# FFN stages of a two-layer hybrid block: another order of the weight splits and low parts on GpSimd, of a tile's turn on TensorE and its norm on VectorE, and its high part cast by ScalarE

## The chip, the cores and the metric

One Trainium2 chip, one core of it. The metric is the device time of one execution in microseconds (us), the median of three runs. TensorE, VectorE, ScalarE, GpSimd and SyncE are called PE, DVE, ACT, POOL and SP in the profile's rows; PEld is TensorE's loading of its stationary operand. SP only issues transfers here.

## The reference

A block of two layers over 1024 latent tokens and 256 context tokens of width 1024. The first part of a layer (three kinds of attention) isn't touched. The second part is the feed-forward sublayer (FFN), hidden width 2816, which ends in a norm; the next layer's input is then normalised and modulated:

```
def swiglu_sublayer(h, shift, scale, gate, w_g, w_u, w_d, g, b):
    u = modulate(h, shift, scale)
    f = (jax.nn.silu(u @ w_g) * (u @ w_u)) @ w_d
    return post_norm(h, f, gate, g, b)          # layer_norm(DN_ALPHA * h + gate * f, g, b)

# next layer: modulate(h, m[0], m[1]) = ln_plain(h) * (1 + m[1]) + m[0]
```

Layer 0 does this for all 1280 tokens (10 tiles of 128), layer 1, the last, for the 1024 latent ones (8 tiles), and has no next layer.

## The kernel before, in words

**Products.** Every matrix product is made of three fp32r products: each operand is split into a high part (a cast to fp32r) and a low part (the value minus its high part), and high x high, high x low and low x high are summed in PSUM (lines 131 to 133, in `product`). So each tile of weights, 128x1024 floats, is loaded by SP into one of two slots of `ring_raw` (line 2555), cast by ACT into one of three slots of `ffn_whi` (line 2634), and subtracted by POOL into `ffn_wlo` (line 2758). Both are called `split` in the code, and run in one fixed order, the list `order`. The load of a tile of weights waits for POOL's split two places earlier in that list; ACT's cast waits until PE is through with the tile three places earlier.

**Stage.** `swiglu` runs 22 groups q (G = 11 per pass, two passes over the weights). A pass takes one set of tokens: the first 768 (layer 0) or 512 (layer 1), the second the last 512. A group takes 256 hidden columns: two halves f, each with a gate tile (`GATE[f]`) and an up tile (`UPPER[f]`) of weights, and two tiles of the down product (`DOWN[0]`, `DOWN[1]`). PE runs in each group: gate and up of half 0, the down product of the group before (`down(q - 1)`, which waits for both of its splits), gate and up of half 1. The gate goes through silu on ACT (2642), is multiplied by up on DVE (2926) and split by POOL into hidden high and low parts (2765, 2767). The down products of 4 tiles x 2 halves are added into `y` by DVE (2934, 2938), through two PSUM banks `ffn_acc`; PE waits when DVE is behind in emptying them.

**Norms.** The tiles of the first pass are complete when the second begins, and are normalised beside it, one in each of the groups G + 1, 2, 4, 5, 7, 8 (layer 0; six tiles) or G + 1, 2, 4, 5 (layer 1; four): `norm_tile(q)` names it. Groups G + 1, 4, 7 are called here the first of a pair, G + 2, 5, 8 the second. The steps of tile k:
- DVE `residual(k)`: y times gate (2894), plus the residual (2900), statistics (2875, 2877); `shifted(k)`: minus the mean, times gain (2908), reciprocal (2883), times that plus bias (2911), and in layer 0 statistics again; `normalizers(k)` (2883, 2888).
- ACT, between them: two roots (`deviation(k, 0)` and `(k, 1)`, 2648), and in layer 0 `normalize(k)` into `ffn_x` (2656).
- PE (layer 0): `turn(k)`, eight transposes (2810), then ACT `modulate(k)`, eight activations (2661), DVE `high_part(k)` (2919), POOL `low_part(k)` (2772) into the next stage's operand `second_uhi`, `second_ulo`. `normalize(k + 1)` waits for `low_part(k)`, since both use `ffn_x`.

Two further tiles, from the stage before, are normalised in groups 0 and 1 of each stage (`late_norm` on DVE, lines 2942 to 2966, `late_low_part` on POOL, 2753).

**Where each step stands.** The order on each engine is written out by hand, in one loop over q per engine. Before the change: DVE runs in group q the high part of the tile of group q - 1, then residual, shifted and normalizers of its own tile, then the multiplication of half 0, the eight additions of the down product and the multiplication of half 1. POOL runs the low part (late or not) of the tile before, then the split of `DOWN[1]` of group q - 1, then `GATE[1]`, hidden, `UPPER[1]`, the next group's first two splits, hidden and `DOWN[0]`. PE turns the tile between the down product and half 1. ACT runs both roots and `normalize` ahead of the casts of half 1, and `modulate` behind the cast of the next group's `GATE[0]` and ahead of the silu of half 1. SP's order of loads, residual loads (2563) and stores (2569, which wait for `h_done`) is not touched.

The wait that PE has at the head of the down product:

```
pe.wait_ge(*split_done(weight(q, DOWN[1])))
for n, (c, tt, at) in enumerate(tiles_of(q)):
    pe.wait_ge(hid_ready, unit(q, 1, c) + 1)
    for half in range(2):
        y = y_count(q, n, half)
        if y > 2:
            pe.wait_ge(y_added, y - 2)
```

Of the kernel before, what the change touches and what calls it, by code (L numbers as in the profile page):

```python
# [22 lines left out]
P = 128  # L23
LAYERS = 2
D = 1024
KT = D // P
# [2392 lines left out]
def swiglu(nc, t, res, layer, last):  # L2419
    with nc.cleanup_on_exit(), ExitStack() as ctx:  # L2420
# [73 lines left out]
        def x_of(k):  # L2494
            return xs[(k - NT) % 2] if k >= NT else x
# [48 lines left out]
        def norm_tile(q):  # L2544
            return group_of.index(q - G) if q - G in group_of else None
# [76 lines left out]
        def _(act):  # L2622
# [35 lines left out]
            def modulate(k, parts=range(KT)):  # L2658
# [3 lines left out]
                                       scale=scale[:, stream(k), i:i + 1], bias=shift[:, stream(k), i:i + 1])  # L2662
                m.then_inc(u_done, 1)

            def late_deviation(k, j):
                act.wait_ge(late_mean_done, 2 * k + j + 1)
                if k:
                    act.wait_ge(late_rs_done, 2 * (k - 1) + j + 1)
                act.activation(late_sd[:, j:j + 1], late_mean[:, j, 1:2], ACT.Sqrt, bias=eps[:, 0:1]).then_inc(late_sd_done, 1)
# [21 lines left out]
            for q in range(Q):  # L2691
                k = norm_tile(q)
                turning = k is not None and not last
                silu(q, 0)
                if 0 < q < Q - 1:
                    split(q - 1, DOWN[1])
                if q < LATE:
                    if q:
                        late_deviation(q, 0)
                    late_deviation(q, 1)  # L2700
                    late_normalize(q)
                if k is not None:
                    deviation(k, 0)
                if turning:
                    deviation(k, 1)
                    normalize(k)
                split(q, GATE[1])
                split(q, UPPER[1])
                if q + 1 < Q:
                    split(q + 1, GATE[0])  # L2710
                if q < LATE:
                    late_modulate(q)
                if turning:
                    if k == 0:
                        act.wait_ge(one_plus, 1)
                    modulate(k)
                silu(q, 1)
                if q + 1 < Q:
                    split(q + 1, UPPER[0])
                if q < Q - 2:  # L2720
                    split(q, DOWN[0])
            for q in range(Q - 2, Q):
                split(q, DOWN[0])
                split(q, DOWN[1])

            def high_part(k):
                at = slice(all_tiles[k] * P, (all_tiles[k] + 1) * P)
                act.wait_ge(u_done, k + 1)
                if k == NT + NL - 1:
                    act.wait_ge(u_rest, 1)  # L2730
                act.copy(uhi[:, :, at], x_of(k)[:, :].rearrange("p (k n) -> p k n", k=KT)).then_inc(u_hi, 1)

            for m in range(NL):
                k = NT + m
# [12 lines left out]
        def _(pool):  # L2747
# [27 lines left out]
            if not last:  # L2775
                for st in range(2):
                    for dst, at in ((shift, 0), (scale, 1)):
                        pool.dma_start(dst[:, st, :], t["mod"][layer + 1, 1 - st, at * D:(at + 1) * D].rearrange("(k p) -> p k", p=P)).then_inc(const_in, 16)
            for q in range(Q):
                if 0 < q <= LATE:  # L2780
                    late_low_part(q - 1)
                if not last and norm_tile(q - 1) is not None:
                    low_part(norm_tile(q - 1))
                if 0 < q < Q - 1:
                    split(q - 1, DOWN[1])
                split(q, GATE[1])
                hidden(q, 0)
                split(q, UPPER[1])
                if q + 1 < Q:
                    split(q + 1, GATE[0])  # L2790
                    split(q + 1, UPPER[0])
                else:
                    split(q - 1, DOWN[0])
                    split(q - 1, DOWN[1])
                hidden(q, 1)
                if q < Q - 2:
                    split(q, DOWN[0])
# [4 lines left out]
        def _(pe):  # L2802
# [49 lines left out]
            for q in range(Q):  # L2852
                if q == G:
                    pe.wait_ge(late_lo, LATE)
                gate_and_up(q, 0)
                if 0 < q < Q - 1:
                    down(q - 1)
                if q < LATE:
                    late_turn(q)
                if norm_tile(q) is not None and not last:  # L2860
                    turn(norm_tile(q))
                gate_and_up(q, 1)
            down(Q - 2)
            down(Q - 1)
            if not last:
# [5 lines left out]
        def _(dve):  # L2871
# [29 lines left out]
                dve.wait_ge(summed, k + 1)  # L2901
                statistics(k, 0)

            def shifted(k):
                y = Y[:, all_tiles[k], :]
                dve.wait_ge(ln_in, 32)
                dve.wait_ge(mv_done[0], k + 1)
                dve.scalar_tensor_tensor(y, y, mv[:, 0, 0:1], lng[:, :], ALU.subtract, ALU.mult).then_inc(centered, 1)  # L2908
                inverse(k, 0)
                dve.wait_ge(centered, k + 1)  # L2910
                dve.scalar_tensor_tensor(y, y, rstd[:, 0:1], lnb[:, :], ALU.mult, ALU.add).then_inc(h_done, 1)  # L2911
                if not last:
                    dve.wait_ge(h_done, k + 1)
                    statistics(k, 1)

            def high_part(k):
                at = slice(all_tiles[k] * P, (all_tiles[k] + 1) * P)
                dve.wait_ge(u_done, k + 1)
                dve.tensor_copy(uhi[:, :, at], x[:, :].rearrange("p (k n) -> p k n", k=KT)).then_inc(u_hi, 1)

            def multiply(q, f):
                for c, (t0, tn) in enumerate(chunks_of(q, f)):
# [47 lines left out]
            for q in range(Q):  # L2970
                k = norm_tile(q)
                if q < LATE:
                    late_norm(q)
                if q == LATE and not last:
                    dve.wait_ge(const_in, 64)
                    dve.tensor_scalar(scale[:, :, :], scale[:, :, :], 1.0, None, ALU.add).then_inc(one_plus, 1)
                if not last and norm_tile(q - 1) is not None:
                    high_part(norm_tile(q - 1))
                if k is not None:
                    residual(k)  # L2980
                    shifted(k)
                    if not last:
                        normalizers(k)
                multiply(q, 0)
                if 0 < q < Q - 1:
                    for n in range(len(tiles_of(q - 1))):
                        accumulate(q - 1, n)
                multiply(q, 1)
            for n in range(len(tiles_of(Q - 2))):
                accumulate(Q - 2, n)  # L2990
# [6 lines left out]
            for m in range(NL + 1):  # L2997
                k = NT + m
                if m < NL:
                    accumulate(Q - 1, m)  # L3000
                if m and not last:
                    normalizers(k - 1)
                if m < NL:
                    residual(k)
                    shifted(k)
                if 0 < m < NL and not last:
                    if m == NL - 1:
                        normalizers(k)
                        low_part(k - 1)
                        break  # L3010
                    low_part(k - 1)
# [161 lines left out]
```

## Time and profile before

| what | value |
|---|---|
| the three runs | 3757.8, 3759.4, 3764.65 us; median 3759.4 us |
| span of the profiled execution, first to last instruction | 3757.6 us |
| busy, share of the span | PE 91%, PEld 75%, DVE 44%, POOL 43%, ACT 39% |
| mean granted TensorE clock over the span | 0.955 of full speed |

The profiled execution is shown by its span; the time around it (launch and end) has no row of its own, and the median of the runs is 1.8 us above that span. The two FFN stages are the stretches from about 1110 to 2100 us (layer 0; its second pass from 1660 us on) and from about 2990 us to the end (layer 1). A row of the timeline reads: start and duration in us, engine, line and operation, what it writes and reads, the number of instructions merged, and in brackets how long the engine was idle before it and what ended that. A row of a stretch gives each engine's busy time and number of instructions in it, the granted clock, and the share and rate of the transfers. Matmul ends are modelled, and spans on POOL are rough.

### The profile page before, as it was taken

The numbers are of one execution on the slowest core, as the hardware profiler recorded it, in microseconds if no ns is written. First come the engines' busy times: TensorE is split into PE (matmuls) and PEld (weight loads), VectorE is DVE, ScalarE is ACT, GpSimd is POOL, SyncE is SP. The second block draws the span as 40 slices with busy tenths as digits, with TensorE's granted clock in tenths as the row PEclk, the third lists the DMA queues.
The fourth block names the chain that finished last, engine by engine and source line by source line (L and its number), as shares of the span: only waits on it lengthen the run. The fifth ranks groups of instructions, "written<-read, shape, count | busy, mean of one in ns | idle before, by whom it ended". The sixth has DMA issues, their size and how long they took to land. (4 is left out here: it accounts for less than half of the span.)

```text
span 3757.6 us, 52063 instructions
## 1 busy us (share of the span) xinstructions
PE 3418.3 (91%) x20432; PEld 2826.1 (75%) x20432; DVE 1635.7 (44%) x2527; ACT 1452.5 (39%) x2346; POOL 1612.1 (43%) x1002
## 2 busy tenths in 40 slices
PE   5998987989789999999998799888897899999996
PEld 4987885666578888887776688786665778888885
DVE  4045546856562122224443218548664622224414
ACT  4151766855343111113332333558753432222221
POOL 3011425933235344346654202338632365556652
PEclk8999996989999999999999899998998999999998
DMA  5243501455442111223323234521454332233332
GB/s 208 81 146 139 148 24 54 89 175 167 146 124 98 66 62 64 66 68 113 117 96 106 96 109 151 168 57 53 118 150 150 124 123 96 96 97 117 118 101 84
DMA packets 209630, 409.86 MB, mean 109 GB/s; under 512 B 20192, under 2 KB 114752, under 8 KB 208896
## 3 DMA queue, kind: packets, MB, share of 16 engines
q1 hardware_dynamic: 187344, 381.22, 32.0%
q10 hardware_dynamic: 20480, 21.32, 1.8%
q0 software_dynamic: 1584, 4.24, 0.3%
q8 instruction: 154, 2.52, 0.3%
q14 instruction: 68, 0.56, 0.0%
HBM read 331.20 MB, written 75.51 MB: 108 GB/s over the span
## 5 line engine op out<-in xcount | busy, mean ns | idle before, releaser
L2758 POOL TENSOR_TENSOR ffn_wlo<-ring_raw,ffn_whi 128x1024 fp32r<-128x1024 f32 x262 | 638.0, 2443 | 702.3 <-ACT ffn_whi L2634 701.5
L2634 ACT CAST ffn_whi<-ring_raw 128x1024 fp32r<-128x1024 f32 x264 | 273.0, 1051 | 833.1 <-PE ffn_acc L133 469.4
L2926 DVE TENSOR_TENSOR ffn_silu<-ffn_up,ffn_silu 128x512 f32<-128x512 f32 x110 | 70.1, 637 | 879.9 <-PE ffn_up L133 866.9
L131 PE MATMUL ffn_acc<-ffn_whi,ffn_hhi 128*128 128x512 f32 x792 | 318.2, 402 | 49.5 <-DVE y L2938 24.6
L2938 DVE TENSOR_TENSOR y<-ffn_acc,y 128x512 f32<-128x512 f32 x360 | 248.1, 691 | 252.3 <-PE ffn_acc L133 252.3
L131 PE MATMUL ffn_gate<-second_uhi,ffn_whi 128*128 128x512 f32 (+1 forms) x880 | 326.9, 371 | 22.0 <-DVE ffn_wlo L2969 20.9
L132 PE MATMUL ffn_gate<-second_ulo,ffn_whi 128*128 128x512 f32 (+1 forms) x880 | 325.8, 370 | 0.0
L133 PE MATMUL ffn_gate<-second_uhi,ffn_wlo 128*128 128x512 f32 (+1 forms) x880 | 325.3, 370 | 0.0
L131 PE MATMUL ffn_up<-second_uhi,ffn_whi 128*128 128x512 f32 (+1 forms) x880 | 324.0, 368 | 0.0
L132 PE MATMUL ffn_up<-second_ulo,ffn_whi 128*128 128x512 f32 (+1 forms) x880 | 323.9, 368 | 0.0
L133 PE MATMUL ffn_up<-second_uhi,ffn_wlo 128*128 128x512 f32 (+1 forms) x880 | 323.7, 368 | 0.0
L132 PE MATMUL ffn_acc<-ffn_wlo,ffn_hhi 128*128 128x512 f32 x792 | 316.7, 400 | 0.0
L133 PE MATMUL ffn_acc<-ffn_whi,ffn_hlo 128*128 128x512 f32 x792 | 315.1, 398 | 0.0
L131 PEld LDWEIGHTS ffn_acc<-ffn_whi,ffn_hhi 128*128 128x128 f32 x792 | 153.3, 194 | 87.8 <-issue 28.8
L2373 DVE TENSOR_SCALAR_CACHE_REDUCE diff_scores<-diff_scores 128x1280 f32<-128x1280 f32 (+1 forms) x144 | 196.8, 1382 | 25.1 <-PE diff_scores L2234 19.9
L131 PEld LDWEIGHTS ffn_gate<-second_uhi,ffn_whi 128*128 128x128 f32 x880 | 167.0, 190 | 50.7 <-DVE ffn_wlo L2969 21.4
L2642 ACT ACTIVATE ffn_silu<-ffn_gate 128x512 f32<-128x512 f32 x110 | 61.2, 558 | 370.5 <-PE ffn_gate L133 370.4
L2351 POOL TENSOR_TENSOR diff_w<-diff_w,diff_e 128x1280 f32<-128x1280 f32 (+1 forms) x72 | 192.0, 2667 | 6.0
L2303 ACT ACTIVATE diff_e<-diff_scores,diff_negmax 128x1280 f32<-128x1280 f32 (+1 forms) x144 | 178.6, 1240 | 36.9 <-DVE diff_scores L2373 35.9
L1914 POOL TENSOR_SCALAR swa_p<-swa_p,swa_rden 128x640 f32<-128x640 f32 (+1 forms) x144 | 107.3, 764 | 193.3 <-DVE swa_rden L2089 193.3
L132 PEld LDWEIGHTS ffn_gate<-second_ulo,ffn_whi 128*128 128x128 f32 x880 | 167.1, 190 | 28.0
L133 PEld LDWEIGHTS ffn_gate<-second_uhi,ffn_wlo 128*128 128x128 f32 x880 | 167.1, 190 | 28.0
(332 smaller groups left out, 7979.0 us busy)
## 6 DMA issues: line engine op xcount, KB each, us to landing
ring_raw<-w_ffn_dram SPq DMA_DIRECT2D x264, 512.0 KB, 3.5
swa_ada_w<-w_ada_dram SPq DMA_DIRECT2D x20, 2048.0 KB
gla_kq<-proj_scratch SPq DMA_DIRECT2D x32, 320.0 KB, 7.7
local_qhl<-heads_scratch SPq DMA_DIRECT2D x36, 256.0 KB, 7.6
norm_attention_mix<-mix_scratch SPq DMA_DIRECT2D x18, 512.0 KB, 5.3
h_mid_scratch<-late_h SPq DMA_DIRECT2D x18, 512.0 KB, 5.2
first_ada_w<-w_ada_dram SPq DMA_DIRECT2D x4, 2048.0 KB
in_w_raw<-w_in_dram SPq DMA_DIRECT2D x15, 512.0 KB, 5.7
```

The costliest lines, as they stand in the source:

```text
L131: pe.matmul(out, st_hi, mv_hi, start=start, stop=False)
L132: pe.matmul(out, st_hi, mv_lo, start=False, stop=False)
L133: return pe.matmul(out, st_lo, mv_hi, start=False, stop=stop)
L1914: pool.tensor_scalar(pr[:, m % RING, j, 0:keys], pr[:, m % RING, j, 0:keys], rden[:, m % RING, j:j + 1], 1.0, ALU.mult, ALU.mult).then_inc ...
L2303: act.activation(E[:, r % 4, c, 0:keys], SC[:, c, 0:keys], ACT.Exp, bias=ng[:, c:c + 1], scale=-1.0, accum_out=den[:, c, tile_of(i, r), r ...
L2351: pool.tensor_tensor(w, w, E[:, u % 4, 0, 0:keys], ALU.add).then_inc(w_done, 1)
L2373: dve.tensor_scalar(SC[:, c, 0:keys], SC[:, c, 0:keys], -scale, 3e38, ALU.mult, ALU.min, accum_out=ng[:, c:c + 1]).then_inc(neg_done, 1)
L2634: act.copy(whi[:, w % 3, :], raw[:, w % 2, :]).then_inc(w_hi, 1)
L2642: act.activation(sg[:, n % 2, 0:tn], GT[:, n % 2, 0:tn], ACT.Silu).then_inc(silu_done, 1)
L2758: pool.tensor_tensor(wlo[:, w % 3, :], raw[:, w % 2, :], whi[:, w % 3, :].bitcast(F32), ALU.subtract).then_inc(w_ready, 1)
L2926: dve.tensor_tensor(sg[:, n % 2, 0:tn], UP[:, n % 2, 0:tn], sg[:, n % 2, 0:tn], ALU.mult).then_inc(mul_done, 1)
L2938: dve.tensor_tensor(Y[:, tt, cols], ACC[:, half, :], Y[:, tt, cols], ALU.add).then_inc(y_added, 1)
```

## The change: what it does

- **POOL:** the split of `DOWN[1]` of the group before stands first in a group, ahead of both kinds of low part; the low part of a normalised tile moves behind the split of `UPPER[1]`.
- **DVE:** `shifted` gives up its first step (2908), now `centre`, which stays behind `residual`, ahead of the multiplication of half 0. The rest of `shifted`, and `normalizers`, move behind the additions of the down product. The high part is gone from DVE.
- **ACT:** the second root and `normalize` move behind the cast of the next group's `GATE[0]`; `modulate` behind the silu of half 1 and the cast of the next `UPPER[0]`; the high part follows it on ACT, ahead of the cast of `DOWN[0]`.
- **PE:** the turn moves behind gate and up of half 1.

```diff
@@ ScalarE
+            def high_part(k):
+                at = slice(all_tiles[k] * P, (all_tiles[k] + 1) * P)
+                act.wait_ge(u_done, k + 1)
+                if k == NT + NL - 1:
+                    act.wait_ge(u_rest, 1)
+                act.copy(uhi[:, :, at], x_of(k)[:, :].rearrange("p (k n) -> p k n", k=KT)).then_inc(u_hi, 1)
...
                 if k is not None:
                     deviation(k, 0)
-                if turning:
-                    deviation(k, 1)
-                    normalize(k)
                 split(q, GATE[1])
                 split(q, UPPER[1])
                 if q + 1 < Q:
...
                 if q < LATE:
                     late_modulate(q)
                 if turning:
+                    deviation(k, 1)
+                    normalize(k)
+                silu(q, 1)
+                if q + 1 < Q:
+                    split(q + 1, UPPER[0])
+                if turning:
                     if k == 0:
                         act.wait_ge(one_plus, 1)
                     modulate(k)
-                silu(q, 1)
-                if q + 1 < Q:
-                    split(q + 1, UPPER[0])
+                    high_part(k)
                 if q < Q - 2:
                     split(q, DOWN[0])
@@ GpSimd
             for q in range(Q):
+                if 0 < q < Q - 1:
+                    split(q - 1, DOWN[1])
                 if 0 < q <= LATE:
                     late_low_part(q - 1)
-                if not last and norm_tile(q - 1) is not None:
-                    low_part(norm_tile(q - 1))
-                if 0 < q < Q - 1:
-                    split(q - 1, DOWN[1])
                 split(q, GATE[1])
                 hidden(q, 0)
                 split(q, UPPER[1])
+                if not last and norm_tile(q - 1) is not None:
+                    low_part(norm_tile(q - 1))
                 if q + 1 < Q:
                     split(q + 1, GATE[0])
                     split(q + 1, UPPER[0])
@@ TensorE
                 if q < LATE:
                     late_turn(q)
+                gate_and_up(q, 1)
                 if norm_tile(q) is not None and not last:
                     turn(norm_tile(q))
-                gate_and_up(q, 1)
@@ VectorE
-            def shifted(k):
+            def centre(k):
                 y = Y[:, all_tiles[k], :]
                 dve.wait_ge(ln_in, 32)
                 dve.wait_ge(mv_done[0], k + 1)
                 dve.scalar_tensor_tensor(y, y, mv[:, 0, 0:1], lng[:, :], ALU.subtract, ALU.mult).then_inc(centered, 1)
+
+            def shifted(k):
+                y = Y[:, all_tiles[k], :]
                 inverse(k, 0)
...
-            def high_part(k):
-                at = slice(all_tiles[k] * P, (all_tiles[k] + 1) * P)
-                dve.wait_ge(u_done, k + 1)
-                dve.tensor_copy(uhi[:, :, at], x[:, :].rearrange("p (k n) -> p k n", k=KT)).then_inc(u_hi, 1)
...
-                if not last and norm_tile(q - 1) is not None:
-                    high_part(norm_tile(q - 1))
                 if k is not None:
                     residual(k)
-                    shifted(k)
-                    if not last:
-                        normalizers(k)
+                    centre(k)
                 multiply(q, 0)
                 if 0 < q < Q - 1:
                     for n in range(len(tiles_of(q - 1))):
                         accumulate(q - 1, n)
+                if k is not None:
+                    shifted(k)
+                    if not last:
+                        normalizers(k)
                 multiply(q, 1)
...
                 if m < NL:
                     residual(k)
+                    centre(k)
                     shifted(k)
```

## Rows read from the trace of the kernel before

**Rows 1.** The page: the span and each engine's busy time
```profile
span 3757.6 us, 52063 instructions
PE 3418.3 (91%) x20432; PEld 2826.1 (75%) x20432; DVE 1635.7 (44%) x2527; ACT 1452.5 (39%) x2346; POOL 1612.1 (43%) x1002
```

**Rows 2.** PE's waits, 1690 to 2000 us: releaser, total us, times, longest
```profile
PE ffn_acc L131 <- POOL ffn_wlo L2758: 9.7, 3, 3.2
PE ffn_acc L131 <- DVE y L2938: 2.9, 2, 1.5
PE ffn_acc L131 <- DVE y L2934: 1.5, 1, 1.5
```

**Rows 3.** PE's waits, 3020 to 3060 us (layer 1)
```profile
PE ffn_acc L131 <- POOL ffn_wlo L2758: 4.1, 1, 4.1
```

**Rows 4.** Stretches: down products behind a gap, one without, 10 us around 1695 us
```profile
1733.63:1746.30 12.67, 12.67 (x49) 10.20 (x50) 5.48 (x9) 2.18 (x2) 4.22 (x3) 0.87 0.50 167
...
1946.81:1960.70 13.89, 13.89 (x48) 11.13 (x49) 5.48 (x9) 2.18 (x2) 4.21 (x3) 0.78 0.23 77
3034.12:3046.78 12.66, 12.65 (x48) 10.20 (x49) 5.49 (x9) 2.18 (x2) 4.22 (x3) 0.87 0.40 126
1768.94:1779.82 10.88, 10.88 (x49) 9.01 (x48) 5.53 (x8) 1.06 (x1) 4.25 (x3) 1.00 0.29 99
...
1690.00:1700.00 10.00, 8.55 (x38) 6.82 (x37) 8.66 (x11) 5.16 (x7) 4.47 (x2) 1.00 0.43 157
```

**Rows 5.** Timeline of DVE, first group of a pair (1684 to 1702 us)
```profile
1689.39 2.92 DVE L2908 SCALAR_TENSOR_TENSOR y<-y,ffn_mv,ffn_lng 128x1024 f32<-128x1024 f32 x1
...
1695.69 1.29 DVE L2875 BATCH_NORM_STATS2 ffn_stats<-y 128x6 f32<-128x512 f32 x2
...
1698.46 1.28 DVE L2934 COPY y<-ffn_acc 128x512 f32<-128x512 f32 x2
```

**Rows 6.** Timeline of POOL, second group of a pair (1718 to 1736 us)
```profile
1723.56 3.39 POOL L2758 TENSOR_TENSOR ffn_wlo<-ring_raw,ffn_whi 128x1024 fp32r<-128x1024 f32 x1
1726.91 3.38 POOL L2772 TENSOR_TENSOR second_ulo<-ffn_x,second_uhi 128x1024 fp32r<-128x1024 f32 x1
1730.26 3.32 POOL L2758 TENSOR_TENSOR ffn_wlo<-ring_raw,ffn_whi 128x1024 fp32r<-128x1024 f32 x1
```

**Rows 7.** Timeline of PE: the first matmul behind each of two gaps (two queries)
```profile
1699.29 0.47 PE L131 MATMUL ffn_acc<-ffn_whi,ffn_hhi 128*128 128x512 f32 x1 [1.45 <-DVE y L2934]
...
1733.63 0.50 PE L131 MATMUL ffn_acc<-ffn_whi,ffn_hhi 128*128 128x512 f32 x1 [3.24 <-POOL ffn_wlo L2758]
```

**Rows 8.** Timeline of POOL, first group, splits behind the down product
```profile
1708.90 4.75 POOL L2758 TENSOR_TENSOR ffn_wlo<-ring_raw,ffn_whi 128x1024 fp32r<-128x1024 f32 x2 [4.35 <-ACT ffn_whi L2634]
```

**Rows 9.** Timeline of ACT, the same pair of groups (1706 to 1736 us)
```profile
1709.68 2.90 ACT L2661 ACTIVATE ffn_x<-ffn_tr,ffn_shift,ffn_scale 128x128 f32<-128x128 f32 x8
1712.61 1.28 ACT L2642 ACT_TABLE_LOAD   x1
...
1719.54 1.06 ACT L2634 CAST ffn_whi<-ring_raw 128x1024 fp32r<-128x1024 f32 x1 [3.65 <-PE ffn_up L133]
1724.98 0.60 ACT L2642 ACTIVATE ffn_silu<-ffn_gate 128x512 f32<-128x512 f32 x1 [4.38 <-PE ffn_gate L133]
...
1733.69 1.25 ACT L2656 ACTIVATE ffn_x<-y,ffn_nmu,ffn_rstd 128x1024 f32<-128x1024 f32 x1 [0.42 <-DVE ffn_nmu L2888]
```

**Rows 10.** Timeline of PE: the turn, between the down product and half 1
```profile
1707.58 1.03 PE L2810 MATMUL ffn_tr<-ident,ffn_x 128*128 128x128 f32 x8
1708.37 0.48 PE L131 MATMUL ffn_gate<-second_uhi,ffn_whi 128*128 128x512 f32 x1
```

**Rows 11.** Timeline of DVE, layer 0's tail, POOL idle (2049 to 2058 us)
```profile
2053.61 1.28 DVE L2908 SCALAR_TENSOR_TENSOR y<-y,ffn_mv,ffn_lng 128x1024 f32<-128x1024 f32 x1
```

**Rows 12.** Timeline of POOL, layer 1, group 1 (3022 to 3037 us)
```profile
3028.42 2.37 POOL L2753 TENSOR_TENSOR second_ulo<-ffn_x,second_uhi 128x1024 fp32r<-128x1024 f32 x1
3030.75 3.33 POOL L2758 TENSOR_TENSOR ffn_wlo<-ring_raw,ffn_whi 128x1024 fp32r<-128x1024 f32 x1
```

More of the change, by code:

```diff
@@ L2724, in _ @@
                 split(q, DOWN[1])
-            def high_part(k):
-                at = slice(all_tiles[k] * P, (all_tiles[k] + 1) * P)
[L2728 to L2731, printed above, removed]
             for m in range(NL):
@@ L2914, in shifted @@
                     statistics(k, 1)
-            def high_part(k):
-                at = slice(all_tiles[k] * P, (all_tiles[k] + 1) * P)
-                dve.wait_ge(u_done, k + 1)
-                dve.tensor_copy(uhi[:, :, at], x[:, :].rearrange("p (k n) -> p k n", k=KT)).then_inc(u_hi, 1)
             def multiply(q, f):
```

## The prediction

> **What bounds the kernel now.** I read the page first: PE is busy for 91% of the span and DVE, POOL and ACT for less than half of it each [rows 1], so in the FFN stages only what makes PE wait, or slows its clock, costs time. The tables of PE's waits, taken per stretch, come next, because the change moves work in the second pass of layer 0, in that of layer 1, and in the first groups of both stages. Between 1690 and 2000 us of layer 0 PE waits six times: three times for POOL's split of a down tile, 9.7 us in all, and three times for DVE to empty a bank of `ffn_acc`, 2.9 + 1.5 = 4.4 us [rows 2]. In layer 1, whose tiles are not turned, the one wait near the change is 4.1 us, in group 1, again for POOL's split [rows 3]. There is nothing else to win: the waits in the two tails belong to code whose order stays.
>
> The timelines show why. **Gap A**, first group of a pair: DVE finishes the whole norm before it multiplies half 0, and only then empties the first two banks, together, at 1698.46 [rows 5]; PE has filled both and stands for 1.45 us, till 1699.29 [rows 7]. **Gap B**, second group of a pair: POOL splits `DOWN[0]` from 1723.56, makes the low part of the tile before from 1726.91, and comes to `DOWN[1]` only at 1730.26 [rows 6]; PE starts the down product at 1733.63, 3.24 us late [rows 7], so it was due at 1730.39. **Gap C** in layer 1 is the same with the late low part between the two splits, 3028.42 to 3030.75 [rows 12].
>
> The clock comes on top. The down product takes 10.88 us at clock 1.00; behind gaps B and C it takes 12.67, 13.89 and 12.66 us, at mean clocks of 0.87, 0.78 and 0.87 [rows 4]; the fourth, behind the second gap B, is like the first, that is, part of it at the lower level of 1.2 GHz. Behind gap A the stretch has clock 1.00 [rows 4].
>
> **Part 1, DVE's order (gap A).** Only residual and centring stay ahead of the multiplication. In the first group centring began at 1689.39 and took 2.92 us [rows 5], so DVE is free at 1692.3, 2.7 us before PE ends the up product (1699.29 - 1.45 is where it stopped, 1697.8, with two of eight banks filled, 1.4 us each: 1695.0). Gap A goes: 3 x 1.45 = **4.4 us**. Its cover is those 2.7 us; if it is gone, the gap can only come back up to its old 1.45.
>
> What moves behind the additions is a chain: a reciprocal, the bias step, like centring 1.28 us with POOL idle and up to 2.9 beside it, statistics 1.29 [rows 5, 11], a root and small steps (some 1.3 us: between the statistics' end, 1697.0, and the additions at 1698.46 the old order has 1.5 us, half a multiplication among them), normalize 1.25 [rows 9]. From the end D of the down product it takes 0.9 for the last addition and the reciprocal, 1.28 to 2.9 for the bias step, 1.3 and 1.3, and 1.25: normalize ends at D + 6.0 to D + 7.7, with two idle hops of 0.4 at D + 8.2; then a table load of 1.28, which ACT had before too, and silu 0.60 end at D + 10.1 [rows 9]. PE ends half 1 at D + 11 (two products of 5.5), the multiplication needs silu then, and PE turns the tile then. Both fit, with 0.9 and 2.8 us over. `UPPER[0]` of the next group is cast behind that silu and split by D + 13.7; PE needs it at D + 17.3. Costed at nothing. The turn costs PE 0.8 us (1707.58 to 1708.37, [rows 10]) in either place. In the second group normalize also waits for POOL's low part of the tile before: `UPPER[1]` till D + 4.7, low part till D + 7.1 or 8.1; normalize would end a microsecond or so later, and silu at about D + 11, at the limit but hidden again, as the down product of this half is 11 us further on.
>
> A queue to look at is POOL's `UPPER[1]` split, now beside DVE's bias step. It starts 1.2 us behind D and takes 2.4 us (4.75 for two, [rows 8]), 3.39 beside DVE [rows 6]: 1708.90 + 3.39 = 1712.3. PE no longer turns before half 1, so needs it at 1707.6 + 5.5 = 1713.1 less a weight load, about 1712.8. It fits by 0.5 us; both ends are 0 and, if two DVE steps get ahead of it, 0.5 us per tile, 3 us in all; I take 0. SP: the store waits for `h_done`, which comes some 9 us later than now, at D + 4, still before SP reaches it behind the load of `DOWN[1]` of the next group (issued after D + 13). The residual load, behind `summed`, comes no later. POOL's queue carries no transfer here.
>
> Beside this the Trainium skill has a rule that would speak against putting the bias step beside a split: "SBUF — State Buffer", section "Who interferes with whom", says that VectorE instructions with two SBUF inputs and GpSimd's reads exclude each other for the whole instruction. The trace agrees in kind (a centring of 1.28 us takes 2.92, a split of 2.4 takes 3.39). By its bound a split waits one full DVE step, 2.4 + 1.28 = 3.7 us, and ends at 1712.6, still no gap, so the sum would be the same by it.
>
> **Part 2, POOL's order and the high part on ACT (gap B).** The low part leaves the place between the splits, 3.38 us. But `DOWN[0]` now starts later. The turn ends with half 1: transposes end some 0.25 us after PE starts the next gate product at 1719.34, so 1719.6. Then on ACT modulate 2.90, the high part 1.05 (the price of an ACT cast of the same shape, [rows 9]; on DVE it was shorter, but it is gone there), the cast of `DOWN[0]` 1.06: done at 1724.7, not 1720.60 [rows 9]. Silu at 1724.98 keeps its time, and the cast of `DOWN[1]` behind it, done at about 1726.6. POOL splits `DOWN[0]` from 1724.7, `DOWN[1]` behind it. Lower end, both free: 1724.7 + 4.75 = 1729.5, no gap. Upper end, both beside DVE: 1724.7 + 2 x 3.39 = 1731.5, a gap of 1.1 us against 1730.39. DVE starts its norm steps of the second group about a microsecond earlier than now (half 1 ends before the turn) and without the high part; centring begins near 1724.5 and holds POOL once, after which DVE is idle until 1730.6. So one split of 3.39 and one of 2.4: 1730.5, a gap of 0.1 to 0.3. I take 0.3 for each of three pairs: 9.7 - 0.9 = **8.8 us**. In groups behind a pair DVE has no norm, so 1729.5 and no gap. First groups of a pair have no turn before them.
>
> **Part 3, the late low part (gap C).** `DOWN[1]` starts at 3028.42 in its place and ends at 3030.8 to 3031.2 [rows 12]; PE was due at 3034.12 - 4.12 = 3030.0. A gap of 0.8 to 1.2 stays; I take 0.9: **3.2 us**. The late low part then ends at about 3034.1, where the second late tile's normalize stood anyway. In layer 0 the first pass is 768 wide and has no such gap; nothing there.
>
> **Part 4, the clock.** Gaps of 1.45 us left the clock at 1.00; the 3.24 and 4.12 gaps did not. With none left above 1.3, the excess goes: 1.79 + 1.76 + 3.01 + 1.78 = **8.3 us** [rows 4]. Its ends are 0 (the clock falls elsewhere) and 8.3.
>
> Sum: 4.4 + 8.8 + 3.2 + 8.3 = 24.7 us off 3757.6, so a span of 3732.9; the median lies 1.8 above that span, so **3734.7 us**.
>
> **Rivals.**
> (1) The gains of the gaps come, those of the clock don't: the clock can fall in other stretches of both tails, where it already changes often. 3734.7 + 8.3 = 3743. For it: the third product lost 3.0 us and the others 1.8, so a drop has no fixed price; against it: the second pass has no fall of the clock except behind these gaps. 0.13.
> (2) The down splits are late in five groups behind a norm tile or more: both splits are slowed, and ACT's cast is late. A gap of 1.1 in six groups costs 6.6 - 0.9 = 5.7: 3740. If the clock falls after each as well, 6 x 1.8 more: 3751, at the border of no change. 0.12 for the first, 0.05 for the second.
> (3) On the other side, slower. One mechanism: `modulate` and the high part, now in ACT's queue ahead of the cast of `DOWN[0]`, delay the pair of splits in all six groups behind a norm tile. Its price, at the longest gap seen and its clock, is 4.12 + 1.78 = 5.9 us each, 35.4 in all, against 25.6 won: 3759.4 + 9.8 = 3769. It decides from 4.3 us per group with the clock, a gap of 2.5: `DOWN[1]` ready at 1732.9 or later, 2.4 us after my estimate. For it: the cast of `DOWN[0]` does move 4.1 us; against it: POOL was busy for 3 of these with other work, and what is taken away is 3.4. 0.04.
> (4) DVE's order has no effect (gap A is limited by something else) and gap B is only halved, with the clock half won: 2.2 + 1.6 + 4.9 + 4 = about 9 to 11 us less than my sum: 3745 to 3750. 0.06.
>
> A difference of 0.2%, 7.5 us, is about what a measurement of this kernel can tell from no change. **How the numbers follow:** my forecast and its small variations, 3730 to 3739, 0.60; the rivals as given; 3751 to 3767 in all 0.06. Faster by over 0.2% (below 3751.9) 0.90, same 0.06, slower 0.04. The range: below, no gap left at all and a tail that is a little kinder, 3729; above it takes in rivals 1 and 2 without the clock's return, 3746.
>
> **What would show it.** In the second pass of layer 0 PE's table of waits should lose DVE's rows altogether and show POOL's split at under 1.3 us in all; the ten-microsecond stretches of that pass should all have clock 1.00. In rows of ACT a cast of 1.05 into `second_uhi` should stand behind eight activations, just after PE's next gate begins. POOL's second down split should end within 0.5 us of the end of the up product. Layer 1's group 1 should show a gap near 0.9 at full clock. The prediction is wrong if a new releaser stands in PE's table (ACT's normalize before the turn, or POOL's split of `UPPER[1]`), or if the clock falls in the pass.

## The result, and the profile after

The changed kernel takes 3738.0 us (median of 4 runs, 3733.6 to 3739.3) against 3759.7 (median of 4, 3757.8 to 3764.7): ratio 0.994, 95% interval 0.9926 to 0.9954, so 0.5 to 0.7% faster, 21.7 us by the medians. 3734.7 us was forecast, in a range of 3729 to 3746.

The page after, beside [rows 1]: the same number of instructions, and a span 20.8 us shorter.

```profile
span 3736.8 us, 52063 instructions
PE 3413.0 (91%) x20432; PEld 2822.8 (76%) x20432; DVE 1614.5 (43%) x2521; ACT 1456.5 (39%) x2352; POOL 1612.6 (43%) x1002
```

DVE has six instructions fewer, ACT six more: the high parts. PE's table of waits for 1660 to 2003 us, the second pass of layer 0 up to its tail, has no row at all; it had six waits, 9.7 + 4.4 us [rows 2]. Stretches of the kernel after, two down products (first and second group of the first pair) and the whole of that pass:

```profile
1692.82:1703.73 10.91, 10.91 (x50) 9.02 (x49) 5.53 (x8) 1.05 (x1) 4.25 (x3) 1.00 0.41 145
1726.38:1737.26 10.88, 10.88 (x49) 9.01 (x48) 5.53 (x8) 1.05 (x1) 4.24 (x3) 1.00 0.58 197
...
1660.00:2003.00 343.00, 343.00 (x1538) 284.10 (x1536) 126.53 (x179) 123.82 (x166) 215.26 (x108) 1.00 0.34 111
```

PE is busy for 343.00 of 343.00 us at clock 1.00, and the second groups' down product takes 10.88 us, where the kernel before had 12.67 to 13.89 [rows 4]. Where the time came from is read from PE's first matmul of each stage. First the kernel before (start of layer 0's FFN stage, of layer 1's projection, of layer 1's FFN stage), then the one after:

```profile
1111.57 0.79 PE L131 MATMUL ffn_gate<-second_uhi,ffn_whi 128*128 128x512 f32 x1 [10.52 <-DVE ffn_wlo L2969]
...
2103.05 0.79 PE L131 MATMUL in_acc<-second_uhi,in_w_whi 128*128 128x512 f32 x1 [7.31 <-DVE in_w_wlo L1152]
...
2992.54 0.79 PE L131 MATMUL ffn_gate<-second_uhi,ffn_whi 128*128 128x512 f32 x1 [10.40 <-DVE ffn_wlo L2969]
```

```profile
1108.95 0.80 PE L131 MATMUL ffn_gate<-second_uhi,ffn_whi 128*128 128x512 f32 x1 [10.50 <-DVE ffn_wlo L2968]
...
2078.70 0.79 PE L131 MATMUL in_acc<-second_uhi,in_w_whi 128*128 128x512 f32 x1 [7.30 <-DVE in_w_wlo L1152]
...
2975.63 0.79 PE L131 MATMUL ffn_gate<-second_uhi,ffn_whi 128*128 128x512 f32 x1 [10.37 <-DVE ffn_wlo L2968]
```

The differences of these starts, with the end of the span as the end of the last stage, in us:

| stretch | before | after | difference |
|---|---|---|---|
| up to layer 0's FFN stage | 1111.6 | 1108.9 | -2.6 |
| layer 0's FFN stage | 991.5 | 969.8 | -21.7 |
| layer 1's projection and attention | 889.5 | 896.9 | +7.4 |
| layer 1's FFN stage | 765.1 | 761.1 | -4.0 |

The two stages that the change touches won 25.7 us in this pair of profiles. Two stretches whose code is the same moved by -2.6 and +7.4. A second profile of the kernel before (further down) has 989.3 and 763.9 us for the two stages, and beside that one the change won 19.5 and 2.8, 22.3 us.

Timeline of ACT after, from the turn of the first tile to the next group's root, beside [rows 9]:

```profile
1715.75 2.90 ACT L2661 ACTIVATE ffn_x<-ffn_tr,ffn_shift,ffn_scale 128x128 f32<-128x128 f32 x8 [2.84 <-PE ffn_tr L2811]
1718.68 1.05 ACT L2670 CAST second_uhi<-ffn_x 128x1024 fp32r<-128x1024 f32 x1
1719.64 1.04 ACT L2634 CAST ffn_whi<-ring_raw 128x1024 fp32r<-128x1024 f32 x1
1721.14 0.60 ACT L2642 ACTIVATE ffn_silu<-ffn_gate 128x512 f32<-128x512 f32 x1 [0.46 <-PE ffn_gate L133]
1721.64 1.04 ACT L2634 CAST ffn_whi<-ring_raw 128x1024 fp32r<-128x1024 f32 x1
```

And POOL's two down splits behind it, beside [rows 6]:

```profile
1720.76 5.08 POOL L2759 TENSOR_TENSOR ffn_wlo<-ring_raw,ffn_whi 128x1024 fp32r<-128x1024 f32 x2 [1.34 <-ACT ffn_whi L2634]
```

The pair ends at 1725.84, 0.5 us ahead of the down product at 1726.38. In layer 1's group 1, PE's table of waits (2985 to 3060 us) shows gap C at 0.8 us, and a wait for DVE that was not there before [rows 3]:

```profile
PE ffn_acc L131 <- DVE y L2933: 1.6, 1, 1.6
PE ffn_gate L131 <- POOL ffn_wlo L2759: 1.1, 1, 1.1
PE ffn_acc L131 <- POOL ffn_wlo L2759: 0.8, 1, 0.8
```

(The 1.1 us, in group 0, was there before as well, with 1.0.) In the kernel before, DVE's late norm of that group and its multiplication had ended no sooner than POOL's split, which took until 3034.08 [rows 12]:

```profile
3034.07 0.69 DVE L2926 TENSOR_TENSOR ffn_silu<-ffn_up,ffn_silu 128x512 f32<-128x512 f32 x1
```

### The profile page after: what moved, and what is told of

Read it like the earlier page. It is cut to its first block and busy times, and to the rows that moved or that the text cites. A ratio compares the mean times of both kernels' runs of the same rounds, so it can differ in the third digit from the quotient of the medians.

```text
span 3736.8 us, 52063 instructions
## 1 busy us (share of the span) xinstructions
PE 3413.0 (91%) x20432; PEld 2822.8 (76%) x20432; DVE 1614.5 (43%) x2521; ACT 1456.5 (39%) x2352; POOL 1612.6 (43%) x1002
## 5 line engine op out<-in xcount | busy, mean ns | idle before, releaser
L2373 DVE TENSOR_SCALAR_CACHE_REDUCE diff_scores<-diff_scores 128x1280 f32<-128x1280 f32 (+1 forms) x144 | 196.7, 1383 | 23.6 <-PE diff_scores L2234 18.6
```

Of the source, the lines that this page charges most:

```text
L2373: dve.tensor_scalar(SC[:, c, 0:keys], SC[:, c, 0:keys], -scale, 3e38, ALU.mult, ALU.min, accum_out=ng[:, c:c + 1]).then_inc(neg_done, 1)
```

## The experiments

Stage lengths below are read as in the table above, from one profile each. A time without "a single run" is a median; a ratio is to runs of the kernel before that were timed beside it.

**The low part's place.** The changed kernel, with POOL's order in a group as:

```diff
+                if not last and norm_tile(q - 1) is not None:
+                    low_part(norm_tile(q - 1))
                 if 0 < q < Q - 1:
                     split(q - 1, DOWN[1])
                 ...
                 split(q, UPPER[1])
-                if not last and norm_tile(q - 1) is not None:
-                    low_part(norm_tile(q - 1))
```

> The changed kernel with one part undone: POOL makes the low part of a normalised tile again ahead of the split of DOWN[1], at the head of the next group. Theory (the place of the low part made gap B): in the changed kernel POOL ends DOWN[0] at 1723.5 and DOWN[1] at 1725.8, 0.5 us before PE needs it; 2.4 us more make it late by 1.9 us in the second groups of a pair and, where DOWN[1] ends at 1759.0 for 1759.9, by 1.5 us in the groups behind them: 10 us in all, all of it under POOL's split in PE's waits, the clock perhaps still 1.00. Rival (the high part on ACT and DVE's shorter norm had already cured gap B): no waits, 0 us.

Measured: 3749.0 us, ratio to the kernel before 0.9969 (0.9954 to 0.9983); layer 0's stage 979.3 us, 9.5 more than with the change whole. PE's table of waits, 1660 to 2010 us:

```profile
PE ffn_acc L131 <- POOL ffn_wlo L2759: 8.8, 6, 1.7
```

Six gaps, 1.66 us in the second groups of a pair and 1.28 in those behind them (1.9 and 1.5 expected), at clock 1.00. So the place of the low part made gap B, and with the other parts of the change in force it costs six groups instead of three. That ACT's later cast of `DOWN[0]` has used up POOL's slack there fits the times, but no run moved that cast alone.

**DVE's order.** The changed kernel with:

```diff
                     centre(k)
+                    shifted(k)
+                    if not last:
+                        normalizers(k)
                 multiply(q, 0)
                 ...
-                if k is not None:
-                    shifted(k)
-                    if not last:
-                        normalizers(k)
@@ ScalarE
                     deviation(k, 0)
+                if turning:
+                    deviation(k, 1)
                 split(q, GATE[1])
```

> The changed kernel with DVE's order undone: the whole norm stands again ahead of the multiplication of half 0, with ACT's second root ahead of the casts of half 1 so that DVE can finish. Theory (DVE's order made gap A): the three gaps of 1.45 us of the first groups come back, 4.4 us, and in the second groups, where gap B no longer hides the same chain, up to 1.5 us each more: 4.4 to 9 us. Rival (gap A came from POOL's or ACT's order): no waits of PE for DVE in the second pass, 0 us.

Measured: 3745.5 us, ratio 0.9962 (0.9951 to 0.9974); layer 0's stage 979.5 us, 9.7 more, a little over the 4.4 to 9 expected. PE's waits, 1660 to 2010 us:

```profile
PE ffn_acc L131 <- DVE y L2938: 6.8, 5, 1.5
PE ffn_acc L131 <- DVE y L2934: 1.5, 1, 1.5
```

Gap A returns at 1.45 us in the first groups, and the second groups have one of 1.29 each that gap B had covered: DVE ends the norm, multiplies at 1730.88 and empties the two banks together. The waits sum to 8.3 us of the 9.7; a gap costs about 0.3 us more than its idle time, since the down product around a gap of 1.45 takes 12.61 us, and 10.88 to 10.91 without one.

```profile
1730.88 0.69 DVE L2926 TENSOR_TENSOR ffn_silu<-ffn_up,ffn_silu 128x512 f32<-128x512 f32 x1
1731.49 1.28 DVE L2938 TENSOR_TENSOR y<-ffn_acc,y 128x512 f32<-128x512 f32 x2
```

**POOL's part alone.** The kernel before with:

```diff
+                if 0 < q < Q - 1:
+                    split(q - 1, DOWN[1])
                 if 0 < q <= LATE:
                     late_low_part(q - 1)
                 if not last and norm_tile(q - 1) is not None:
                     low_part(norm_tile(q - 1))
-                if 0 < q < Q - 1:
-                    split(q - 1, DOWN[1])
                 split(q, GATE[1])
```

The low part can't go behind `UPPER[1]` here: ACT's `normalize` of the next tile waits for it and stands ahead of the casts of half 1 in ACT's queue, so the two would wait for each other.

> The kernel before with POOL's part alone, as far as it goes without the others: the split of DOWN[1] first, both kinds of low part behind it, ahead of GATE[1]. Theory (the parts are coupled: gap B hid a second one behind it, DVE's): POOL's waits leave the second pass of layer 0 and with them the lower clock, but the three gaps of 1.45 us of the first groups stay and DVE's norm, now uncovered, costs 1.3 to 2.5 us in each second group; layer 0's FFN stage 979 to 983 us against 991.5, and layer 1's 761 as in the changed kernel. Rival (POOL's order was all of it but gap A): second groups without a gap, 975 us.

Measured: 3746.6 us, ratio 0.9963 (0.995 to 0.9976); layer 0's stage 982.0 us, layer 1's 762.8. PE's waits, 1660 to 2010 us:

```profile
PE ffn_acc L131 <- DVE y L2938: 7.9, 5, 1.7
PE ffn_acc L131 <- DVE y L2934: 1.5, 1, 1.5
```

Gap B became a gap of 1.65 us for DVE in each second group, gap A stayed at 1.47, and the stretch has clock 1.00. POOL's order alone is worth 9.5 us in layer 0's stage and 2.3 in layer 1's, about half of the 25.7 (7.3 and 1.2 of 22.3 beside the second profile of the kernel before); the rest needs DVE's. Layer 1's stage was expected at 761; its gap for DVE, 1.66 us, is there as in the changed kernel.

**The high part's engine.** The changed kernel with the six high parts back on DVE:

```diff
                     modulate(k)
-                    high_part(k)
                 if q < Q - 2:
@@ VectorE
+                if not last and norm_tile(q - 1) is not None:
+                    high_part(norm_tile(q - 1))
                 if k is not None:
                     residual(k)
```

> The changed kernel with the high part of the six tiles of the second pass back on DVE, at the head of the next group. Theory (its move bought nothing by itself): ACT ends the cast of DOWN[0] 1.05 us earlier, DVE starts its norm 0.6 us later, PE still has no wait in the second pass, the time is the same within 1 us. Rival (it was needed, as DVE's cast holds POOL up): POOL's second down split comes late in the second groups, 0.5 us or more each, 1.5 us or more in all.

Measured: 3736.8 us, ratio 0.9933 (0.9912 to 0.9955); layer 0's stage 969.5 us against 969.8, and no wait of PE between 1685 and 2005 us. The move to ACT bought nothing by itself.

**The turn's place.** The changed kernel with:

```diff
+                if norm_tile(q) is not None and not last:
+                    turn(norm_tile(q))
                 gate_and_up(q, 1)
-                if norm_tile(q) is not None and not last:
-                    turn(norm_tile(q))
```

> The changed kernel with the turn put back between the down product and half 1 on PE. Theory (with the norm finished behind the additions the turn had to move too): PE stands from the end of the down product until normalize ends, 5.7 us in the first groups and 8.1 us in the second, 41 us in all, and the clock falls after each, 1.8 to 3.4 us more: 52 to 62 us slower. Rival (a turn is short enough to stand anywhere): within 5 us.

Measured: 3796.4 us, ratio 1.0086 (1.0062 to 1.011); layer 0's stage 1029.6 us, 59.8 more. PE's waits, 1685 to 2005 us, and from the timeline the first tile's turn and the second's:

```profile
PE ffn_tr L2811 <- ACT ffn_x L2656: 41.2, 6, 8.0
```

```profile
1711.06 0.69 PE L2811 MATMUL ffn_tr<-ident,ffn_x 128*128 128x128 f32 x2 [5.73 <-ACT ffn_x L2656]
...
1755.66 0.69 PE L2811 MATMUL ffn_tr<-ident,ffn_x 128*128 128x128 f32 x2 [8.01 <-ACT ffn_x L2656]
```

41.2 us are waiting; the other 18.6 go with a lower clock, 0.93 over 1685 to 2065 us. So DVE's and ACT's new order can't be had without the turn's move. What that move would be worth without them was not run; in the kernel before, PE never waited at the turn [rows 2].

**The late low part.** The changed kernel with:

```diff
+                if 0 < q <= LATE:
+                    late_low_part(q - 1)
                 if 0 < q < Q - 1:
                     split(q - 1, DOWN[1])
-                if 0 < q <= LATE:
-                    late_low_part(q - 1)
```

> The changed kernel with the late low parts back ahead of the split of DOWN[1]. Theory (this alone is what layer 1's stage gained): in group 1 of layer 1 the gap of 4.1 us for POOL's split returns with 1.8 us of clock, and the 0.8 and 1.6 us of the changed kernel go: layer 1's FFN stage 764.5 to 765.5 us against 761.1; layer 0's the same 969.8. Rival (DVE's order gave layer 1 the gain): 761 us.

Measured, a single run: 3739.6 us; layer 1's stage 765.9 us against 761.1, layer 0's 968.7. The gap is back:

```profile
3011.83 0.79 PE L131 MATMUL ffn_acc<-ffn_whi,ffn_hhi 128*128 128x512 f32 x1 [4.12 <-POOL ffn_wlo L2759]
```

The up and the down product around the gap take 22.9 us here, 19.3 with the change whole and 22.4 in the kernel before. So this exchange of two instructions is what layer 1's stage gained; the rest of the 4.8 us lies mostly in the first product of the stage, which took 8.2 us here and 7.1 there and varies so between profiles.

**The kernel before, once more.**

> The kernel before, once more, for a second profile of it. Open is why the changed kernel won 21.7 us in layer 0's FFN stage and 4.0 us in layer 1's, 25.7 in all as forecast, and yet its span is only 20.8 us shorter: layer 1's projection and attention, which the change does not touch, took 896.9 us for 889.5 (894 to 901 in the other variants), with more time at the lower clock. Theory (scatter: the first profile of the kernel before was a lucky one there): this stretch takes 893 to 900 us here too. Rival (the change shifts something in it): 888 to 891 us again.

Measured, a single run: a span of 3753.8 us; projection and attention 891.0 us, so the first profile was no lucky one, and the theory's 893 to 900 fell. In the order of its length, that stretch took 889.0 (the kernel before with POOL's part), 889.5 and 891.0 (the kernel before), 892.3 (late low part back), 892.9, 894.1, 894.4, 895.1 and 895.5, 896.9 (the change), 898.9 and 900.8 us in twelve profiles. Its instructions are the same in all. The nine kernels that hold the change, some with one part undone or with something added, scatter by 8.5 us among themselves. But the three that don't hold it are the three shortest, with a mean of 889.9 us against 895.7; if the change had no effect there, such an order would come up once in 220 times. So a shift of some 6 us by the change is likely, and how it would come about is open. The time at the lower clock in the stretch goes from 87 to 109 us, and 4.9 of the 7.4 us between the first profile before and the one after arise between 214 and 305 us behind its start.

**One norm more in the new order.** The changed kernel, and the second late tile's norm in group 1 treated as the change treats the others:

```diff
                 if q == 1:
-                    late_norm(q)
+                    late_norm_head(q)            # statistics, centring
                 ...
                 multiply(q, 0); accumulate(q - 1, n) for all n
+                if q == 1:
+                    late_norm_rest(q)            # bias, statistics, normalizers
@@ ScalarE: late_deviation(1, 1), late_normalize(1) behind the cast of GATE[0] of the next group,
@@          late_modulate(1) behind the cast of UPPER[0]; TensorE: late_turn(1) behind gate_and_up(1, 1)
```

> The changed kernel, and the second late tile's norm in group 1 ordered as the change orders the others: centring ahead of the multiplication of half 0, the rest behind the additions, ACT's second root and normalize behind the casts, the turn behind half 1. Theory (the 1.6 us gap that the changed kernel shows in group 1 of layer 1, for DVE, is gap A once more, which gap C had hidden): it goes, the 0.8 us for POOL's split stay, layer 1's FFN stage 759.5 us against 761.1, layer 0's as it was, 969.8. Rival (POOL's late low part causes it through the port): it stays, 761 us.

Measured, a single run: 3734.3 us; layer 1's stage 762.5 us, not 759.5, layer 0's 968.8. PE's waits, 2985 to 3060 us:

```profile
PE ffn_tr L2855 <- ACT ffn_x L2682: 1.3, 1, 1.3
PE ffn_acc L131 <- POOL ffn_wlo L2764: 1.2, 2, 0.7
```

The wait for DVE is gone as the theory had it, but the turn now waits 1.3 us for ACT's normalize. A gap was exchanged for another. SP and ACT show why normalize is late:

```profile
3020.24 0.33 SPq L2579 DMA_DIRECT2D h_mid_scratch<-late_h  x1
3020.61 8.72 SPq L2555 DMA_DIRECT2D ring_raw<-w_ffn_dram  x3
```

```profile
3025.46 1.05 ACT L2634 CAST ffn_whi<-ring_raw 128x1024 fp32r<-128x1024 f32 x1 [6.28 <-DMA ring_raw<-w_ffn_dram]
3026.42 0.29 ACT L2676 ACTIVATE ffn_late_sd<-ffn_late_mean,ffn_eps 128x1 f32<-128x1 f32 x1
```

SP's store of the late tile waits for DVE's bias step, which now ends at 3020.21, and it stands ahead of the next group's load of `GATE[0]` in SP's queue. So the load, the cast behind it and the second root behind the cast are late, although DVE had the root's input ready at 3021.8. The move made a wait on a queue that nobody had reordered.

**The last down split.** The changed kernel, and in the last group of each stage:

```diff
+        def w_high(w):                           # w_low alike, with spare[:, 1, :] and wlo
+            return spare[:, 0, :] if own and w == 6 * Q - 1 else whi[:, w % 3, :]
@@ ScalarE, split: the slot of its own needs no wait for PE
-                if w >= 3:
+                if w >= 3 and not (own and w == 6 * Q - 1):
@@ GpSimd
             split(Q - 1, DOWN[0])
-            split(Q - 1, DOWN[1])
+            if own:                              # own = last
+                split(Q - 1, DOWN[1])
@@ VectorE, behind the additions of group Q - 2
+            if not own:
+                w = weight(Q - 1, DOWN[1])
+                dve.wait_ge(w_hi, w + 1)
+                dve.wait_ge(w_ready, w - 1)
+                dve.tensor_tensor(w_low(w), raw[:, w % 2, :], w_high(w).bitcast(F32), ALU.subtract).then_inc(w_ready, 1)
```

> The changed kernel and one thing more, in the last group of each stage, whose last down split PE waits 3.55 us for, as its slot only comes free when the down product before it ends: in layer 0 DVE makes that low part (1.22 us for 2.4), in layer 1, where memory is free, the tile gets slots of its own and is split ahead. Theory (that wait lies on the path and nothing else is late there): 3.55 becomes 2.4 us in layer 0 and 0 in layer 1, with up to 3.4 us of clock: 4.7 to 8 us less than the changed kernel. Rival (DVE's residual and norm of the last tiles end last in either case, so PE only waits later): 1 us or less in layer 1.

Measured: 3729.9 us (3727.1 to 3734.5), ratio to the kernel before 0.9916 (0.9903 to 0.993); layer 0's stage 968.4 us (-1.4), layer 1's 757.3 (-3.8), 5.2 in all, where 4.7 to 8 were expected. In layer 0 the wait is now for DVE:

```profile
2020.63 0.50 PE L131 MATMUL ffn_acc<-ffn_whi,ffn_hhi 128*128 128x512 f32 x1 [2.39 <-DVE ffn_wlo L3005]
```

In layer 1, PE's waits between 3690 and 3740 us, first after the change, then here: the split's row is gone and DVE's is as long as it was.

```profile
PE ffn_acc L131 <- DVE y L2937: 9.1, 2, 5.7
PE ffn_acc L131 <- POOL ffn_wlo L2759: 3.6, 1, 3.6
```

```profile
PE ffn_acc L131 <- DVE y L2948: 9.1, 2, 5.7
```

**Both additions.**

> The changed kernel with both additions, the second late tile's norm ordered like the others and the last down split of each stage made by DVE (layer 0) or in slots of its own (layer 1). Theory (they add): layer 0's stage 968.4 us as with the second alone, layer 1's 757.3 less 1.6, 755.7; the median 3725 to 3730 us. Rival (the late tile's later steps delay the first pass of layer 0 or 1 elsewhere): no gain over the second addition alone, 3730 us or more.

Measured: 3727.3 us (3724.6 to 3732.0), ratio 0.9921 (0.9908 to 0.9934); stages 966.9 and 756.5 us. Its interval and that of the last split alone overlap, so what the late tile's order adds is within the measurement. Either version is about 0.8% faster than the kernel before. Over the changed kernel the ratios give 0.2%, but their intervals touch, so that step rests on the stages (1.4 and 3.8 us less with the last split).

## Why the prediction was right

**Bound, gaps and rows.** That only PE's waits and its clock count in these stages held: putting the six high parts back on DVE changed the stage by 0.3 us.

**Part 1, gap A: 4.4 us of waits, right.** DVE ended centring at 1690.4 and then stood idle for 2.7 us, the cover that was named. Timeline of DVE after, beside [rows 5]:

```profile
1687.44 2.92 DVE L2909 SCALAR_TENSOR_TENSOR y<-y,ffn_mv,ffn_lng 128x1024 f32<-128x1024 f32 x1
1693.09 0.69 DVE L2925 TENSOR_TENSOR ffn_silu<-ffn_up,ffn_silu 128x512 f32<-128x512 f32 x1 [2.74 <-PE ffn_up L133]
1694.41 0.69 DVE L2933 COPY y<-ffn_acc 128x512 f32<-128x512 f32 x1 [0.62 <-PE ffn_acc L133]
```

The gaps cost 5.1 us and not 4.4: the down product around each took 12.59 to 12.62 us and now takes 10.88 to 10.91. What I had not said is that the same order made a second gap in the second groups, of 1.3 to 1.65 us, which lay under gap B. Undoing DVE's order costs 9.7 us, not 4.4: the part is worth more once POOL's is in force. The forecast was not hurt, since it took both changes at once and asked for what is late next.

**The chain behind the additions** was sized too long in the first groups (and its worst case was summed wrongly: 7.7 and two hops of 0.4 make 8.5, not 8.2): normalize ended 5.7 us behind the down product, not 8.2, since the bias step ran ahead of POOL's split at 1.29 us. In the second groups it waited 2.8 us for POOL's low part, as said, and ended 8.1 behind (8.2 and about one more expected):

```profile
1744.25 1.25 ACT L2656 ACTIVATE ffn_x<-y,ffn_nmu,ffn_rstd 128x1024 f32<-128x1024 f32 x1 [2.81 <-POOL second_ulo L2773]
```

**POOL's `UPPER[1]` split** ended with 0.9 us to spare (1705.06 + 3.21 = 1708.27, needed at 1709.2). DVE's bias step began 0.34 us before it and ended at 1706.0; from there the split took 2.26 us, about its free 2.4. The Trainium skill states in "SBUF — State Buffer", section "Who interferes with whom", that a VectorE instruction with two inputs in SBUF and a GpSimd one that reads SBUF share a port by an exclusive lock. The trace agrees that the split got on only when the bias step had ended, and centring shows it from the other side: begun at 1687.44 beside a split that ended at 1689.27, it ended at 1690.36, 1.1 us later.

**Part 2, gap B: 8.8 us forecast, 9.7 of waits found, 10.2 with the 0.2 us that each cost beyond its idle time.** The cast of `DOWN[0]` came just where it was put (modulate 2.90, high part 1.05, cast 1.04), but the two splits took 5.08 us and not 5.8: DVE's centring, 1719.93 to 1721.22, was all but over when the first began at 1720.76. The price of ACT's high part was real and covered, and not needed: rival 3 had its delay right (the cast came 4.1 us later in the frame of the old timeline) and its effect wrong.

**Part 3, gap C: 3.2 us forecast for the gap and 1.8 for its clock; the up and the down product around it took 3.0 less.** The step of this part that failed: I asked what POOL's order leaves and not what DVE's does. Gap C had covered a gap for DVE's late norm, 1.61 us, the same pattern as gap A, visible in the old rows only as DVE's chain ending where POOL's split did. By the idle times that is 4.1 + 1.8 - 0.8 - 1.6 = 3.5 us; the two products took 22.4 us before and 19.3 after. The stage won 4.0, as its first product took 7.1 us and not 7.8, which varies so between profiles. So this part was priced at 5.0 and is worth 3.0.

**Part 4, the clock: 8.3 us, right.** The pass has clock 1.00 throughout. In layer 0's stage 21.7 us were won: 5.1 by gap A, 10.2 by gap B, 6.6 in the three slowed down products, less 0.2 that the stage's first products and its tail took more. The 3.0 us of clock behind the third gap are no fixed price: in the second profile of the kernel before that product took 12.51 us, 1.6 too many, behind the same gap.

**The sum.** The terms that the change accounts for make 5.1 + 10.2 + 6.6 + 3.0 = 24.9 us for the 24.7 forecast. That it comes so close is partly luck: parts 1 and 2 were 2.1 too low and part 3 was 2.0 too high. Beside the second profile the two stages won only 22.3.

**Rivals.** Rival 1 did not come in the stages that it named. But something like it may have come outside: the 7.4 us that attention took more in this profile are why the span is 3736.8 and not 3732.9, and by the twelve profiles some 6 of them may be the change's own doing. The forecast has no term for these stretches. The median, 3.3 us above the forecast, is of the size of either. Rival 4's sum doesn't come out: its four terms make 12.7 us, so the time by it is about 3747, which lies in the 3745 to 3750 it gives, while its "9 to 11 us less" does not.

## What to carry to other kernels

Behind a wait there can be a second one of nearly the same length, on another engine, that the first one covers. Before pricing its removal, follow every engine's chain to the instant at which the bound engine could have gone on; where two end together, neither alone is worth the gap. And of several moves made together some only carry the others: here the turn had to move so that the norm could, while the cast's new engine was not needed. A moved step also carries what waits for it on a queue of its own, as the store of the late tile did with the load behind it.

## What the runs showed that I had not expected

A gap of 1.2 to 1.7 us on PE never lowered the clock in these stages (over 40 cases in the runs). Every one of 2.39 us or more that began at the full clock did: 2.39 twice, in the two runs with the last split on DVE, 3.23 or 3.24 six times, 3.55 in the tails, 3.75 once, 4.12 twice. The price of the same gap of 3.2 us went from 1.6 to 3.0 us. Between 1.7 and 2.39 us there is no case. Stretches of identical code differ by 12 us between profiles (889.0 to 900.8), and stages of the same kernel by 2.2 and 1.1 (989.3 and 991.5, 763.9 and 765.1). So a gain of 20 us in a kernel of 3750 is better read from the stages that were touched, with a second profile of the kernel before beside it, and the stretches that were not touched have to be read as well: they may have moved too.
